# Pooling means of a hybrid encoder layer: from banded matmuls on TensorE to shifted fp32 adds on VectorE

## The reference, cut to what matters

```python
h = rms_norm(x, g_pre) * (1.0 + scale) + shift           # scale, shift, gate from c @ ada_w
u_pool, q, k, v, z = split(h @ w_in)                     # 1024, 1024, 1024, 1024, 2048 columns
y_pool = multiscale_pool(u_pool, pool_w, pool_scale)     # below
y_ret  = bidir_retention(q, k, v, dec_f, dec_b)          # 8 heads, chunks of 128, forward and backward
out = (concat(y_pool, y_ret) * silu(z)) @ w_out
y = x + gate * rms_norm(out, g_post)
```

## Time and profile before

| | |
|---|---|
| median of 3 runs | 3203.11 us (3199.91 to 3203.42) |
| the profiled execution | 3200.19 us; span of its slowest core 3198.4 us (8 cores: 3188.4 to 3198.4) |
| PE, matmul busy | 3012.1 us, 94% of the span |
| DVE, ACT, POOL busy | 2212.1 (69%), 1258.1 (39%), 1148.8 us (36%) |
| TensorE's granted clock, mean | 0.984 of full speed on that core |
| HBM | 160 GB/s over the span |

### The profile page before, as it was taken

How to read it: one execution, slowest core, us unless ns; L and a number is a source line. 1 busy time by engine, 2 the same in 40 slices (tenths; PEclk the granted TensorE clock), 3 DMA queues, 4 the chain that set the end, 5 groups by cost and what they waited for, 6 DMA issues and landing times.

```text
span 3198.4 us, 51337 instructions; the slowest of 8 cores (3188.4 to 3198.4 us)
## 1 busy us (share of the span) xinstructions
PE 3012.1 (94%) x18160; PEld 1530.4 (48%) x18160; DVE 2212.1 (69%) x2510; ACT 1258.1 (39%) x1995; POOL 1148.8 (36%) x1007
## 2 busy tenths in 40 slices
PE   0699999999999999999979999999999999999997
PEld 0344444444444444444435555555555555555553
DVE  5557666666666566666357787778777877787774
ACT  3444433334344343443223444444444443444442
POOL 1433343334333232323113434444444443444443
PEclk9899999999999999999989999999999999999999
DMA  7855665456756665554677777777778777877774
GB/s 151 206 154 143 174 159 153 141 153 164 184 157 174 161 174 144 162 145 127 207 188 198 221 204 198 209 221 204 204 205 226 204 205 202 230 204 205 200 204 130
DMA packets 508200, 583.34 MB, mean 182 GB/s; under 512 B 328614, under 2 KB 353190, under 8 KB 500012
## 3 DMA queue, kind: packets, MB, share of 16 engines
q1 hardware_dynamic: 503340, 554.88, 62.7%
q0 software_dynamic: 4032, 20.97, 4.5%
q10 hardware_dynamic: 576, 4.19, 0.4%
HBM read 307.80 MB, written 202.91 MB: 160 GB/s over the span
## 4 chain that ended last, share of the span: by engine, by line
PE 88%; DVE 4%; DMA 4%; issue 2%; ACT 1%; POOL 0%; SPq 0%; DVEq 0%; POOLq 0%; ACTq 0%
PE psum L839 58%; PE psum L1349 21%; PE psum L1282 4%; DVE hT L827 2%; PE psum L992 1%; PE psum L1239 1%; PE psum L1315 1%; PE psum L935 1%; DMA yT<-yr 1%; DMA xn<-x 1%; DMA ypS<-yo 1%; PE psum L1055 1%; DMA xn<-wv 1%; DVE psum L905 0%; DMA QT<-qo 0%
## 5 line engine op out<-in xcount | busy, mean ns | idle before, releaser
L1289 POOL TENSOR_TENSOR rs<-st,mhalf 128x8 f32<-128x8 f32 x96 | 158.7, 1653 | 832.7 <-DVE st L1288 832.7
L839 PE MATMUL psum<-wu,hT 128*128 128x512 bf16 x1536 | 358.5, 388 | 39.8 <-DVE hT L827 37.3
L1349 PE MATMUL psum<-wo,yp 128*128 128x512 bf16 x1536 | 366.2, 382 | 15.0 <-DMA yT<-yr 14.9
L911 POOL TENSOR_TENSOR kb<-kr,kd 128x1024 bf16<-128x1024 bf16 x94 | 178.7, 1901 | 539.2 <-DVE kr L906 539.2
L1349 PE MATMUL psum<-wo,yT 128*128 128x512 bf16 x1536 | 364.7, 380 | 0.0
L904 DVE TENSOR_TENSOR t<-psum,rn 128x1024 f32<-128x1024 f32 x96 | 117.5, 1224 | 351.9 <-PE psum L839 346.7
L839 PE MATMUL psum<-hT,wq 128*128 128x512 bf16 x1536 | 349.7, 381 | 6.4 <-DVE yo L999 6.4
L839 PE MATMUL psum<-wzr,hT 128*128 128x512 bf16 x1536 | 349.6, 381 | 1.3 <-ACT SF L1319 1.3
L839 PE MATMUL psum<-hT,wzp 128*128 128x512 bf16 x1536 | 347.2, 379 | 0.0
L839 PE MATMUL psum<-wv,hT 128*128 128x512 bf16 x1472 | 332.7, 379 | 0.0
L839 PE MATMUL psum<-wk,hT 128*128 128x512 bf16 x1472 | 332.7, 379 | 0.0
(11 more groups left out here) (180 smaller groups left out, 4864.7 us busy)
## 6 DMA issues: line engine op xcount, KB each, us to landing
xn<-x SPq DMA_DIRECT2D x192, 512.0 KB, 5.2
y<-xn SPq DMA_DIRECT2D x96, 512.0 KB, 2.7
hS<-hT SPq DMA_DIRECT2D x24, 1024.0 KB, 5.6
krS<-kr SPq DMA_DIRECT2D x96, 256.0 KB, 2.0
vS<-vA SPq DMA_DIRECT2D x96, 256.0 KB, 5.7
ypS<-yo SPq DMA_DIRECT2D x24, 1024.0 KB, 8.5
hT<-hS SPq DMA_DIRECT2D x24, 1024.0 KB, 7.3
QT<-qo SPq DMA_DIRECT2D x384, 64.0 KB, 2.5
```

Source lines behind the costliest of these rows:

```text
L839: last = e.matmul(pp(p, half * 512, half * 512 + 512), lhs(half, dc), rhs(half, dc), start=(dc == 0), stop=(dc == 7))
L911: pool(lambda e: e.tensor_tensor(out=h3(kb[:, :]), in0=h3(kr[:, :]), in1=bch(kd[:, 1, :]), op=ALU.mult), 2.3, r=[krb, kdb_], w=[kbb])
L1289: pool(lambda e: e.tensor_tensor(out=rs[:, :], in0=st[:, :], in1=mhalf[:, :], op=ALU.pow), 1.65, r=[stb, mhalfb], w=[rsb])
L1349: last = e.matmul(pp(p, half * 512, half * 512 + 512), l_, wo[:, ec, half * 512:half * 512 + 512], start=(ec == 0), stop=(ec == 15))
```

## The change

1. Pooling (`stage_band` becomes `stage_pool`): u is computed with channels on partitions and the 512 tokens of a group on columns, into an fp32 tile with 8 halo columns on each side (`u`, [128, 2, 528], ring of 6). Window sums come from doubling: an add of u and u shifted by one, then adds of the result shifted by 1, 2, 4. The last step scales by 1/w and subtracts u. No matmul and no PSUM is involved. Window 2 takes one subtraction (the factor 0.5 goes into `wu`) and runs on POOL, with its product with silu(z).
2. The scale and shift of h move from DVE to ACT, as 8 instructions of 512 columns in four operations for the whole group, behind all four transposes; transposes and loads are recorded one to two slots earlier than before.
3. Three of `rope_T`'s five instructions move from DVE to ACT.
4. Decay and sum of the backward state: 8 `scalar_tensor_tensor` of 128 x 128 per chunk on DVE, instead of one DVE add and one POOL product.
5. The band matrix's set-up goes; a small table `edge` for the ends of a sequence takes its place.
6. The gate row is computed in eight parts of 128 columns within phase A, each one slot after its weights were loaded (with a cast) straight from the input; `adagS` and `gate_row` go.
7. All four `stage_u` of the last group stand in its slots. `xh` has 3 buffers instead of 4.

The core of the diff:

```diff
-    xh_r = Ring(AC.alloc("xh", [128, 1024], BF16, 4))
+    xh_r = Ring(AC.alloc("xh", [128, 1024], BF16, 3))
...
+    ag_r = Ring(AC.alloc("ag", [128, 8, 128], BF16, 1))
...
-    u_items = AC.alloc("u", [128, 1024], BF16, 10)
-    u_r = Ring(u_items)
+    u_r = Ring(AC.alloc("u", [128, 2, UW], F32, 6))
+    s_r = Ring(AC.alloc("s", [128, 2, UW], F32, 3))
...
-        dve(aff, 1.0, r=[hb, gprb, shfb], a=[hb])
+    def front_affine(k, ra=(0, 4)):
...
+        for d2 in range(4):
+            def aff(e, d2=d2):
+                last = None
+                for dc in (2 * d2, 2 * d2 + 1):
+                    x_ = ht[:, dc, c0:c1]
+                    last = e.activation(out=x_, in_=x_, func=AF.Identity, scale=gpr[:, dc, s:s + 1], bias=shf[:, dc, s:s + 1])
+                return last
+            act(aff, 0.4 + (c1 - c0) / 600.0, r=[gprb, shfb], a=[hb], after=trT[k])
...
-            dve(lambda e: e.tensor_tensor(out=SB[:, :], in0=pp(p), in1=SB[:, :], op=ALU.add), 1.25, r=[p, SBb], w=[SBb])
+                for h in range(8):
+                    x_ = SB[:, h * 128:(h + 1) * 128]
+                    last = e.scalar_tensor_tensor(out=x_, in0=x_, scalar=kd[:, 3, h:h + 1], in1=pp(p, h * 128, h * 128 + 128),
+                                                  op0=ALU.mult, op1=ALU.add)
...
-            pool(lambda e: e.tensor_tensor(out=h3(SB[:, :]), in0=h3(SB[:, :]), in1=bch(kd[:, 3, :]), op=ALU.mult), 2.3, r=[SBb, kdb_], w=[SBb])
...
+        act(lambda e: e.copy(out=u[:, :, 8:8 + G], in_=pp(p).rearrange("p (b t) -> p b t", b=2)), 1.05, r=[p], w=[ub])
...
+            act(lambda e: e.copy(out=n[:, :, 0:8], in_=pp(p).rearrange("p (b t) -> p b t", b=2)[:, :, G - 8:G]), 0.25, r=[p], a=[nb])
+            act(lambda e: e.copy(out=u[:, :, 8 + G:UW], in_=n[:, :, 8:16]), 0.25, r=[nb], a=[ub])
...
-        op("pe", f, 0.62, r=rr, w=[p])
+    def stage_pool(s, g, j, sz, szb):
...
+        if j == 0:
+            m, mb, _ = s_r.next()
+            pool(lambda e: e.tensor_tensor(out=tok(m), in0=u[:, :, 7:7 + G], in1=tok(u), op=ALU.subtract), 2.0, r=[ub], w=[mb])
+        else:
+            a_, ab_, _ = s_r.next()
+            dve(lambda e, a_=a_: e.tensor_tensor(out=a_[:, :, 1:UW], in0=u[:, :, 0:UW - 1], in1=u[:, :, 1:UW], op=ALU.add), 1.25,
+                r=[ub], w=[ab_])
+            for l in range(1, j + 1):
+                d_ = 1 << (l - 1)
...
+                dve(lambda e, a_=a_, b_=b_, d_=d_, lo_=lo_, hi_=hi_: e.tensor_tensor(
+                    out=b_[:, :, lo_:hi_], in0=a_[:, :, lo_ - d_:hi_ - d_], in1=a_[:, :, lo_ + d_:hi_ + d_], op=ALU.add), 1.25,
+                    r=[ab_], w=[bb_])
...
+            dve(lambda e, a_=a_: e.scalar_tensor_tensor(out=tok(m), in0=tok(a_), scalar=1.0 / w_, in1=tok(u), op0=ALU.mult, op1=ALU.subtract),
+                1.25, r=[ab_, ub], w=[mb])
...
+        (dve if j else pool)(lambda e: e.tensor_tensor(out=yo[:, :, 2 * j:2 * j + 2, :].rearrange("p c b t -> p b c t"), in0=v4(tok(m)),
+                                                       in1=sz[:, :].rearrange("p (b c t) -> p b c t", b=2, c=4), op=ALU.mult),
+                             1.3 if j else 2.1, r=[mb, szb], **({"w": [yob]} if j == 0 else {"a": [yob]}))
...
+            kx, jx = (k + 1, 3) if j == 0 else (k + 2, j - 1)
+            if k + 1 < len(groupsA):
+                for n_ in ((0, 1), (2,), (3,), ())[j]:
+                    front_h(k + 1, n_)
+            if kx < len(groupsA):
+                front_x(kx, jx, after=pace)
+            if j == 2 and k + 1 < len(groupsA):
+                front_affine(k + 1)
```

More of the change, by code:

```diff
@@ L731, in build_program @@
     dve(lambda e: e.tensor_scalar_mul(out=rT[:, 1, :], in0=sn[:, 256:768], scalar1=-1.0), 0.45, r=[snb], a=[rTb])
-    for j, w_ in enumerate(POOL_W):
+    dve(lambda e: e.memset(edge[:, :, 0, :], 1.0), 0.1, a=[edgeb])
+    for j in range(1, 4):
+        w_ = POOL_W[j]
         hw = w_ // 2
[L736 to L758, removed]
@@ L761, in build_program @@
+    dve(lambda e: e.reciprocal(out=edge[:, :, 1:4, :],
+                               in_=edge[:, :, 1:4, :]), 0.4, r=[edgeb], w=[edgeb])
     pmod = sc.pair("pmod")
@@ L820, in front_h @@
         xh, xhb, xhk = xhT.pop((k, n_))
[L821 to L828, removed]
-        dve(aff, 1.0, r=[hb, gprb, shfb], a=[hb])
-        if n_ == 3:
+        if n_ == 0:
+            trT[k] = []
+        trT[k] += [dma(ht[:, :, i * 128:(i + 1) * 128], xh[:, :], xhk, r=[xhb], tr=True, late=late, **({"w": [hb]} if n_ == 0 else {"a": [hb]}))]
+    def front_affine(k, ra=(0, 4)):
+        s, g = groupsA[k]
+        ht, hb, hk = hTile[(s, g)]
+        c0, c1 = G - 128 * ra[1], G - 128 * ra[0]
+        for d2 in range(4):
[6 more added lines that the diff above has]
+            act(aff, 0.4 + (c1 - c0) / 600.0, r=[gprb, shfb], a=[hb], after=trT[k])
+        if ra[1] == 4:
             dma(hS[s].ap()[g], fl(ht[:, :, :]), hk, r=[hb], w=[dbuf("h", s, g)])
@@ L1121, in build_program @@
             pend_kv = (s, c, kb, kbb, v, vb)
-            if j == 0 and k + 1 == len(groupsA) and ps == s:
-                stage_u(s, c, ht, hb)
-            stage_band(ps, pg, j, sz, szb)
+            stage_pool(ps, pg, j, sz, szb)
+            if gate_next is not None:
+                gate_next()
+                gate_next = None
             pace = [o for o in sc.ops[-60:] if o.q == "pe"][-1:]
@@ L1131, in build_program @@
                 ci += 1
+            if slot >= 6 and gfc < 8 and slot % 2 == 0:
+                gate_next = gate_cols(gfc, pace)
+                gfc += 1
             wantT = int(NG0 * max(0, slot - 4) / max(1.0, 0.8 * nslots - 4)) + 1
@@ L1149, in build_program @@
         ci += 1
+    if gate_next is not None:
+        gate_next()
+    while gfc < 8:
+        gate_cols(gfc, ())()
+        gfc += 1
     while tgen < NG0:
@@ L1397, in build_program @@
     ht, hb, _ = hTile[(ps, pg)]
-    for c in range(3, -1, -1):
-        if (ps, c) not in uT_:
-            stage_u(ps, c, ht, hb)
-    TG = Area(ag_at)
-    ag = [TG.alloc("ag", [128, 2, 1024], BF16)[0] for _ in range(4)]
-    for k_ in range(4):
-        t, b, nm = ag[k_]
-        dma(fl(t[:, :, :]), adagS.ap()[:, k_ * 2048:(k_ + 1) * 2048], nm, r=[dbuf("adagS")], w=[b])
     for j in range(4):
         sz, szb = stage_zp(ps, pg, j)
-        stage_band(ps, pg, j, sz, szb)
-        if j > 0:
-            stage_q(0, j - 1)
-        if j == 2:
-            gate_row()
+        stage_pool(ps, pg, j, sz, szb)
+        if j > 1:
+            stage_q(0, j - 2)
+    stage_q(0, 2)
     q3 = stage_q(0, 3)
```

145 lines of the change are left out of this document (83 added, 62 removed).

## The result

The changed kernel takes **3115.18 us** (median of three runs) against 3203.11 before: ratio 0.9727 [0.9699, 0.9755]. That is inside the range and 16 us above the forecast of 3099.

A forecast was written before the change was run, and what follows sets the result against it. PE bounds the kernel, matmuls filling 94% of the span. From 3200.2 us: -57.6 - 45.7 + 11 + 1 - 12 = -103.3, so 3096.9; with 2.9 for the median 3099.8, rounded to 3099; range 3070 to 3165.

The forecast's parts named there:

- Band matmuls, 0.60 us per slot: Pooling's matmuls leave PE in 96 slots: 57.6 us saved, a group's PE work falling from 59.39 to 57.0 us.
- Stalls at the group's start gone: PE's waits behind the scale and shift, 2.18 us per group, close through ACT and earlier transposes: at most 45.7 us.
- Rivals 3 and 4: Third: ACT's queue waits for transposes, 3224 us, chance 0.07. Fourth: group-start stalls stay because transposes are late, 3134, chance 0.07.
- DVE: Per group 42.6 us of work plus 3.6 of waits for POOL, 46.2 of 57.0, hidden beneath PE on average.
- The exclusion: DVE instructions with two SBUF inputs and POOL instructions reading SBUF shut each other out: 3.6 us per group on DVE.
- Rival 1: DVE sets the pace, excluded by POOL; PE loses 2.5 us per group behind the k rotation: 3143 us, chance 0.25.
- 11 us for the groups: Allowance for DVE work running over in uneven slots, 0.5 us per group; bounds 0 and 55.
- Gate row: Moved into phase A's slots as 8 runs of at most 0.61 us; 3.62 us leave the transition: +1 us net.
- ACT and POOL: Per-group work: ACT 32.6 of 57.0 us, hidden unless it stands still itself; POOL 14.2 us.
- Between the phases: Transition between phases, PE idle or slow behind DMAs: 0 us change, bounds -10 and +10.
- Start-up: Without the band set-up on DVE, scale and shift begins between 53 and 56: 12 us gained, bounds 0 and 20.
- rival 2: Start-up and transition give nothing: loads set the start's pace, the transition grows by 10: 3121 us, chance 0.09.

The follow-up runs named there:

- the engine alone: Kernel before the change with scale and shift on ACT, chunk by chunk in the old order (8 instructions of 128 columns): ratio 0.9925 (3175 to 3185 us).
- the first run: Changed kernel with four xh buffers of their own for the first two groups, nothing else: 3100 to 3105 us, ratio 0.9681.
- the last kernel: Changed kernel plus four xh buffers in the first two groups, k's decay on ACT from the third group, five wv staging buffers instead of three: ratio 0.966.

## Why the prediction was right, and where it failed

- **Band matmuls, 0.60 us per slot: right.** Groups without a gap went from 59.39 to 57.01 us; 57.0 was forecast. The price from the starts of two neighbouring runs was the right one.
- **Stalls at the group's start gone: right in size, and the reason only half so.** 16 waits became two. The early order with larger instructions and, but for 7.7 us, the engine alone do it. Rivals 3 and 4 fell: between 300 and 1480 us PE has no wait behind the scale and shift.
- **DVE: right.** 507.62 / 11 = 46.1 us per group, 46.2 forecast. A piece of the state took 197.7 / 736 = 0.268 us (0.262 assumed), an undisturbed add of 1050 columns 1.27 (1.25). The exclusion cost (37 x 0.56 + 37 x 0.47 + 25 x 0.51 + 12 x 0.07) / 12.3 = 4.2 us per group, 3.6 forecast, though not spread evenly as the sum took it, but on three of the operations.
- **Rival 1: the mechanism is there, its price was not.** PE lost 6.9 us in six places to it between 300 and 1480 us, 0.3 us per group instead of 2.5. With the residual, 11 us for the groups was about right: the 21 steps took 15.9 us more than 21 x 57.01, and 5 of these are the gate row's.
- **Gate row: right.** Its eight runs cost 0.63 us each (a slot with one takes 14.89 instead of 14.26 us, timeline, 310.67), 5.0 in all, against 3.6 that left the stretch between the phases; there is no wait for their loads.
- **ACT and POOL.** ACT has 31.5 us per group (32.6 forecast), eight scale-and-shift instructions 5.73 us, 0.72 each (0.6 assumed). POOL has 23.5 us, not 14.2: it was summed as if DVE alone paid for the exclusion (last section).
- **Between the phases: 0 forecast, some 3.5 us gained** beyond the work that went (19.9 less 10.4 for three u, 2.4 for the bands and 3.6 for the gate row). The prediction had no line for what went there: PE's wait of 6.4 us for `yo`, behind a store of `ypS` that took 28.46 us (chain of the kernel before, 1573.28). A wait for `scm` of 5.6 us took part of it back. No run took this apart.
- **Start-up: wrong, and the only term of the sum that was far off:** +8.3 us where 12 were to be gained, outside its bounds of 0 to 20. The measured 3115 is nearer to rival 2's 3121 than to the forecast: a start-up that gives nothing came true, though by the first run not for the reason that rival 2 gave, and the rest of it did not. The step that failed was "without the set-up the scale and shift can begin between 53 and 56", from the end of the transposes in the kernel before. That kernel had four buffers `xh`; the change has three, and the sum gave this edit no line. The first run shows it worth 13 us at the second group and 10 to 15 us in all (20 by die 1 later). With four buffers the second group starts 4.6 us earlier than before (161.03 against 165.61), 7 us short of the 12: k came 14.1 us earlier instead of 17, the first group's u 12.2, and the second group's wait grew by 7.6 us (10.85 against 3.22), where the prediction allowed 4.8 for a scale and shift that waits for all four transposes. That kernel as a whole ran in 3100 to 3105 us, within 6 of the forecast.

What stays open: what the start would take if the folding of wv were not late. ACT and POOL, which share it, were found last in turn, but in the changed kernel ACT stood idle for 18.87 us before its last fold (timeline, 122.40), and the chain leads from there to a load of wv (from 104.51, 16.21 us); in the last kernel it leads to one of the pooling weights. No run moved these loads.

## What to carry to other kernels

Give every changed buffer count a line of the sum, also where the ring is far from the edit's purpose: at the start there may be nothing in flight that could cover a missing buffer, and an instruction that waits for one at the head of an in-order queue holds back everything behind it, related or not. When one chain is taken off a start-up, look for the next chain with the same end before booking the gain. And when a change brings two remedies for one stall, try each alone: one of them may not be needed, and may cost time elsewhere. And follow a wait that the profile puts down to an engine one step further: twice here that engine was itself idle, for a store.

## What was not expected of the hardware

By these means POOL pays for the exclusion as DVE does. Its groups by line, 300 to 1500 us, after the change:

```profile
L907 POOL TENSOR_TENSOR kb<-kr,kd 128x1024 bf16<-128x1024 bf16 x82 | 206.8, 2522 | 456.9 <-DVE kr L902 439.3 <-ACT szp L974 13.6 <-DVE s L1001 3.9
L797 POOL TENSOR_TENSOR ssq<-ssq,mhalf 128x1 f32<-128x1 f32 x78 | 84.1, 1079 | 9.6
L796 POOL TENSOR_SCALAR ssq<-ssq 128x1 f32<-128x1 f32 x78 | 71.8, 920 | 55.1 <-ACT xh L795 55.1
```

In the kernel before, the same three took 1.90, 0.59 and 0.24 us in the same stretch. An operation on a single column (L796) grew by 0.68 us on average, as it would if it often found DVE in the middle of an add of 1.25 us; that it was the adds is inferred, no run took them away. With the decay product on ACT it still took 0.59 (same view of that kernel), so about half of the growth stays when POOL's longest operation is gone. The chain of normalisation runs through these two, so a busier DVE also delays ACT, which waited 3.36 us for one of them in a slot (timeline of the changed kernel, 590.05).
